# Two layers of two transformer-like blocks on one Trainium2 core: the recurrence's solution eight heads at a time, and the embedding's end in pieces

## The reference, cut to what matters

```python
def step(state, inp):                      # state S[i (value), j (key)], one per head
    r_t, w_t, k_t, v_t, a_t, b_t = inp
    sa = einsum('bhij,bhj->bhi', state, a_t)
    state = state * w_t[:, :, None, :] + sa[..., None] * b_t[:, :, None, :] + v_t[..., None] * k_t[:, :, None, :]
    y_t = einsum('bhij,bhj->bhi', state, r_t)
    return state, y_t
```

```python
gate = sigmoid(rms_norm_2(h, g[6]) @ ple_w_gate[i])
h = h + rms_norm_2(gate * (p[i] @ ple_w_proj[i]), g[7])
```

## Time and profile before

| | us |
|---|---|
| median of three runs | 2233.99 |
| the profiled execution | 2235.59 |
| its span (first to last instruction shown) | 2233.80 |
| TensorE busy | 2150.1 |
| DVE busy | 1525.5 |
| ACT busy | 1151.3 |
| POOL busy | 354.3 |

### The profile page before, as it was taken

The page is one execution under the profiler, slowest core; times in us unless marked ns, Lnnn a source line. Parts: engine busy times, 40 slices in busy tenths (PEclk is TensorE's granted clock), DMA queues, the critical chain, the costliest instruction groups (busy, mean ns, idle before and its releaser), DMA issues.

```text
span 2233.8 us, 40296 instructions
## 1 busy us (share of the span) xinstructions
PE 2150.1 (96%) x14196; PEld 1837.4 (82%) x14196; DVE 1525.5 (68%) x2386; ACT 1151.3 (52%) x1965; POOL 354.3 (16%) x469
## 2 busy tenths in 40 slices
PE   8999899999999899999999999998999899989997
PEld 7888678888888778888887988887888688868886
DVE  6667956667667866666667757667766785767666
ACT  5546645555456555555545454546544543245445
POOL 1111111112111011121110001111111012301111
PEclk9999999999999999999999999999999999999999
DMA  6555426555555345546556446555655340115653
GB/s 246 195 196 178 134 97 204 186 180 188 187 187 187 104 133 191 193 160 198 187 199 230 147 160 202 193 195 195 198 197 186 128 143 13 60 67 188 197 186 111
DMA packets 104115, 375.61 MB, mean 168 GB/s; under 512 B 11696, under 2 KB 12208, under 8 KB 104016
## 3 DMA queue, kind: packets, MB, share of 16 engines
q1 hardware_dynamic: 104016, 374.24, 50.5%
HBM read 373.15 MB, written 1.05 MB: 168 GB/s over the span
## 4 chain that ended last, share of the span: by engine, by line
PE 83%; DVE 9%; ACT 4%; issue 2%; POOL 1%; DMA 1%; SPq 0%; DVEq 0%; ACTq 0%; POOLq 0%
PE bank L846 27%; PE bank L850 14%; PE bank L186 12%; PE bank L187 11%; PE bank L188 11%; DVE w_lo L180 3%; PE bank L1997 2%; DVE work L1361 1%; PE bank L376 1%; ACT w_hi L173 1%; ACT act L435 1%; DMA work<-pt_dram 1%; ACT work L424 0%; DVE act L545 0%; DVE work L575 0%
## 5 line engine op out<-in xcount | busy, mean ns | idle before, releaser
L846 PE MATMUL bank<-act,w_hi 128*128 128x512 f32 x2816 | 709.9, 394 | 2.2 <-ACT w_hi L173 1.1
L846 PEld LDWEIGHTS bank<-act,w_hi 128*128 128x128 f32 x2816 | 520.1, 190 | 106.0 <-DVE act L545 2.6
L760 DVE TENSOR_TENSOR w_lo<-raw,w_hi 128x1024 fp32r<-128x1024 f32 x432 | 503.0, 1220 | 3.4 <-ACT w_hi L751 0.2
L751 ACT ACTIVATE w_hi<-raw 128x1024 fp32r<-128x1024 f32 x432 | 425.0, 1050 | 2.2
L850 PEld LDWEIGHTS bank<-act,w_lo 128*128 128x128 f32 x2816 | 385.3, 191 | 27.9
L850 PE MATMUL bank<-act,w_lo 128*128 128x256 f32 x2816 | 393.5, 283 | 0.0
L180 DVE TENSOR_TENSOR w_lo<-raw,w_hi 128x1024 fp32r<-128x1024 f32 x248 | 295.2, 1221 | 69.3 <-ACT w_hi L173 69.3
L816 DVE TENSOR_TENSOR work<-bank,work 128x256 f32<-128x256 f32 x176 | 74.9, 426 | 387.2 <-ACT work L778 387.2
L793 POOL TENSOR_TENSOR work<-work,rb 128x256 f32<-128x256 f32 x176 | 130.0, 739 | 1047.8 <-DVE work L813 1045.7
L186 PE MATMUL bank<-w_hi,g_hi 128*128 128x512 f32 x704 | 277.3, 394 | 0.9 <-DVE w_lo L180 0.9
L187 PE MATMUL bank<-w_lo,g_hi 128*128 128x512 f32 x704 | 276.0, 392 | 0.0
(11 more groups left out here) (276 smaller groups left out, 2280.9 us busy)
## 6 DMA issues: line engine op xcount, KB each, us to landing
raw<-w_dram SPq DMA_DIRECT2D x680, 512.0 KB, 4.4
work<-rows_dram SPq DMA_DIRECT2D x13, 512.0 KB, 6.4
work<-rrows_dram SPq DMA_DIRECT2D x5, 512.0 KB, 3.3
x<-x_dram SPq DMA_DIRECT2D x2, 512.0 KB, 4.3
out<-x SPq DMA_DIRECT2D x4, 256.0 KB, 2.1
work<-g_dram SPq DMA_DIRECT2D x1, 640.0 KB, 9.6
work<-dist_dram SPq DMA_DIRECT2D x2, 256.0 KB, 5.5
work<-ws_dram SPq DMA_DIRECT2D x1, 512.0 KB, 8.1
```

Of the source, the lines that this page charges most:

```text
L751: nc.scalar.activation(c.w_hi[:, n % RING, :], c.raw[:, n % RING, :], ACT.Copy).then_inc(c.hi_ready, 1)
L760: nc.vector.tensor_tensor(c.w_lo[:, n % RING, :], c.raw[:, n % RING, :], c.w_hi[:, n % RING, :].bitcast(F32), ALU.subtract).then_inc(c.lo_ ...
L846: nc.tensor.matmul(bank[:, :], c.w_hi[:, slot(m), k * P:(k + 1) * P], c.act[:, k, :, :], start=k == 0, stop=False)
```

## The change

In the solution, eight heads (all of one half) are handled together, in two halves instead of four groups. Only M is kept; its transpose is made in each level by four 128x128 transposes per half (`turned`), copied out of PSUM by ACT, and for t = 0 half of it by DVE. The order of the products is over all four quadrants (`quarters`). The grams of b and of k are taken with r and a together, 128 wide. In the embedding, the first token half of the last unit has a mark of its own, and squares, gains and means move into the embedding's stage; `Finish` becomes a kind of `Join`. The first ACT instruction has another function.

```diff
-        nc.scalar.activation(c.small[:, 508:509], c.ident[:, 0:1], ACT.Copy)
+        nc.scalar.activation(c.small[:, 508:509], c.ident[:, 0:1], ACT.Silu)
```

The embedding, and what it calls (in `Join`; `square_y` is the old loop's activation for one quarter):

```diff
+    def mean_y(self, dve, i):
+        t = self.order[i][0]
+        dve.wait_ge(self.s["y_squares"].sem, self.s["y_squares"].at(i + 1))
+        self.sum_parts(self.y_root, self.y_parts, t, EPS / self.by ** 2, self.s["y_mean"])
+    def gain_y(self, dve):
+        i = self.y_gained
+        self.y_gained += 1
+        t, h = self.order[i]
+        if i == 0:
+            dve.wait_ge(self.c.row_in, 16 * self.gain_number)
+        self.quarter_there(dve, i + 1)
+        nc.vector.tensor_tensor(self.gained(t, h), self.sources(t, h), self.gain[...], ALU.mult)
...
                 product_a(c, pe, first + 2 + h * 4 + k, k, 4, [gate(0, h), gate(1, h)], 0,
-                          join.tile_there if h == 0 else None)
+                          join.tile_there if h == 0 else None, s["first"])
...
         for h in range(2):
-            unit_done(c, act, first + 5 + 4 * h)
             for t in range(NT):
+                if t == 0:
+                    act.wait_ge(s["first"].sem, s["first"].at(h + 1))
+                else:
+                    unit_done(c, act, first + 5 + 4 * h)
                 nc.scalar.activation(..., gate(t, h)[:, :], ACT.Sigmoid, scale=...)
+            for t in range(NT):
+                out.square_y(act)
...
                 nc.vector.tensor_tensor(g, g, proj(t, h)[:, :], ALU.mult).then_inc(quad.sem, 1)
+                if h == 1 and t == 1:
+                    out.mean_y(dve, 2)
+                out.gain_y(dve)
+        out.mean_y(dve, 3)
```

The solution, TensorE's queue:

```diff
+    def gram_two(half, bank, left, done):
+        for q, e, ch in quarters(((0, 0), (1, 1), (0, 1), (1, 0))):
+            rows, tok, p = head_rows[e], chunks[ch], 4 * half + q
+            last = nc.tensor.matmul(two_fours(bank[half][e][:, :])[tok, :, q, :], left[rows, p, tok],
+                                    R.raT[rows, :, p, tok], start=True, stop=True)
+    def first_product(half):
+        for q, e, ch in quarters(((0, 0), (1, 1), (1, 0), (0, 1))):
+            last = nc.tensor.matmul(p_bank[half][ch][head_rows[e], ...], X.low_part[tok, cols], X.m[tok, cols], ...)
+    def turned(half):
+        for q in range(4):
+            last = nc.tensor.transpose(m_bank[half][q % 2][:, ...], X.m[:, q * P:(q + 1) * P], c.ident)
+    def second_product(half):
+        for q, e, ch in quarters(((0, 0), (1, 1), (0, 1), (1, 0))):
+            last = nc.tensor.matmul(m_bank[half][e][tok, ...], X.t[rows, ...], X.p1[rows, ...], ...)
+    def p1_and_t(pe, level, half):
+        pe.wait_ge(*at("lows", step + 1))
+        pe.wait_ge(m_made of the level before, or init_made)
+        first_product(half)
+        if not level:
+            pe.wait_ge(*at("kv_made", half + 1))
+        turned(half)
...
+        gram_low(0)
+        gram_two(0, ab_bank, R.bT, "ab_bank")
+        ...                                     # v_out (t = 0) or the last turns (t = 1)
+        gram_low(1)
+        gram_two(0, k_bank, R.kT, "k_bank")
+        pe.wait_ge(*at("low_copied", 2))
+        gram_two(1, ab_bank, R.bT, "ab_bank")
+        pe.wait_ge(*at("init_masked", 1))
+        gram_two(1, k_bank, R.kT, "k_bank")
+        pe.wait_ge(*at("akrk_made", 1))
+        with_values(0)
+        p1_and_t(pe, 0, 0)
+        pe.wait_ge(*at("akrk_made", 2))
+        with_values(1)
+        p1_and_t(pe, 0, 1)
+        for level in range(LEVELS):
+            for half in range(N):
+                pe.wait_ge(p1_made, t_act, and t_dve if t == 0)
+                second_product(half)
+            if level < LEVELS - 1:
+                for half in range(N):
+                    p1_and_t(pe, level + 1, half)
+        # then per half: 16 products with a (four quadrants), 16 of M with the values
```

The other queues of the solution, in their order:

```diff
+    def copy_products(act, level, half):          # ACT
+        act.wait_ge(*at("p1_bank", step + 1))
+        for ch in range(2):                       # two copies, 256 wide
+            last = nc.scalar.activation(X.p1[:, ch * S:(ch + 1) * S], p_bank[half][ch][:, 0:S], ACT.Copy)
+        act.wait_ge(*at("t_bank", step + 1))
+        for i in range(1 + t):                    # one or two copies, 256 wide
+            last = nc.scalar.activation(t_part(half, i), t_in(half, i), ACT.Copy)
+    # ACT: copy_low x2; per half copy_values (two of 512), copy_products(0); then the levels
+    # ACT, t = 1: head.square(act, 0) after copy_products(2, 0)
+    # POOL: per level and half one mask, 512 wide, after the previous level's p1_bank
+    # DVE, per half: two masks of 512, the identity, two masks of 512; then
+        for level in range(LEVELS):
+            if t == 0:
+                for half in range(N):
+                    dve.wait_ge(*at("t_bank", step + 1))
+                    nc.vector.tensor_copy(t_part(half, 1), t_in(half, 1)).then_inc(s["t_dve"].sem, 1)
+            for half in range(N):
+                dve.wait_ge(*at("m_bank", step + 1))
+                for e in range(2):                # two adds, 256 wide
+                    last = nc.vector.tensor_tensor(m, m, fours(m_bank[half][e][:, 0:S]), ALU.add)
+                if t == 1:
+                    head.while_solving(dve, 2 * step)
+                    head.while_solving(dve, 2 * step + 1)
+    # at the end ACT copies two results of 256 per half, DVE one of 512 (R.base, mark "based")
```

More of the change, by code:

```diff
@@ new lines, in eights, with over8, quarters, gram_low @@
+    def eights(u):
+        return u.rearrange("p (h n) -> p h n", n=CHUNK)
+    def over8(mask):
+        return mask.unsqueeze(1).to_broadcast([P, 8, CHUNK])
+    def quarters(order):
+        return [(q, e, ch) for q in range(4) for e, ch in order]
+    def gram_low(half):
+        for q, e, ch in quarters(((0, 0), (1, 1), (0, 1), (1, 0))):
+            rows, tok, p = head_rows[e], chunks[ch], 4 * half + q
+            last = nc.tensor.matmul(low_bank[half][e][tok, q * CHUNK:(q + 1) * CHUNK], R.aT[rows, p, tok],
+                                    R.bT[rows, p, tok], start=True, stop=True)
+        last.then_inc(s["low_bank"].sem, 1)
@@ new lines, in scalar @@
+        for half in range(N):
+            copy_values(act, half)
+            copy_products(act, 0, half)
+        for level in range(1, LEVELS):
+            for half in range(N):
+                copy_products(act, level, half)
+                if t == 1 and level == 2 and half == 0:
+                    head.square(act, 0)
+        for half in range(N):
+            act.wait_ge(*at("final", half + 1))
+            for ch, tok in enumerate(chunks):
+                last = nc.scalar.activation(R.aT[:, 4 * half:4 * half + 4, tok], fours(p_bank[half][ch][:, 0:S]), ACT.Copy)
```

393 lines of the change are left out of this document (180 added, 213 removed).

## The result

The changed kernel takes 2214.37 us, median of 5 runs (2213.09 to 2216.67), beside 2230.57 (2229.67 to 2234.93) for the kernel before on the same chip: ratio 0.9924, interval 0.9909 to 0.9938, so 17 us less (14 to 20). A second set of runs gave 0.9927 (0.9912 to 0.9942). Forecast were 2212, in 2202 to 2226, by a sum of 21.85 us. The time lies in the range. The profiled execution of before lies 5.0 us above this median of before, and the sum came 5 us short, all of it in the two solutions.

A forecast was written before the change was run, and what follows sets the result against it. TensorE, busy 96% of the span, was taken to bound the kernel. Gains 9.5 + 8.2 + 1.75 + 2.25 + 0.15 = 21.85 us off the profiled 2235.59, which stood 1.60 above the median, gave 2212 us, range 2202 to 2226.

The forecast's parts named there:

- Grams and values: Front of each solution, before the levels: level 1 begins at 15.0 us; gain 3.8 us in the first solution.
- Levels: Levels 1 to 4 of the first solution: 4.16 us each, 16.6 instead of 21.0; gain 4.4 us (3.2 to 6.4).
- End: First solution's end, until the state's first product: 4.0 us instead of 5.37; gain 1.3 us.
- Second solution: The recurrence's second solving: 39.4 us instead of 47.56, levels 18.9 as head work delays DVE's adds; gain 8.2 us.
- Embeddings' ends: Last sigmoid to first add of x in both embeddings: 1.75 and 2.25 us less.
- The gain row: Embedding's end: row wanted at about 1536, there by 1538.3, hidden by a margin of 2 us.
- The wait of 0.15: Kernel start: moving the 1.28 us table load to the start removes TensorE's wait behind it, 0.15 us less.
- The clock: Open term: falls to 1.2 GHz after the first solution (up to 3.5 us) and first embedding (3) may stay or go.
- Rival C: Solutions: quadrants don't overlap as in the grams, products stay at 57 ns, only about 4 us gained: 2230; chance 0.07.
- Rival B: Slower: clock at 1.2 GHz through most of both solutions, decisive from 53% of the time, 2253 at all; chance 0.05.
- Rival A: Clock falls inside the solutions part of the time; a quarter of it costs 10 us: 2222; chance 0.20.
- Rival D: More than the sum: neither clock fall comes back and changes of mode cost nothing: 2203; chance 0.08.

The follow-up runs named there:

- two_pads_32: Changed kernel with 32 more products at the first embedding's end and 32 more in the second solution; 2213.33 us, ratio 0.9905 to the kernel before.
- shift128: Changed kernel with 32 more 64x64 products (128 records) where TensorE waits at the first embedding's end; ratio 0.9914 to the kernel before.
- solution_only: Kernel before with only the new solution; embedding's end, last output and first table unchanged; ratio 0.9950 to the kernel before.
- ends_only: Kernel before with only the embedding's end, last output and first table changed, old solution kept; ratio 0.9978 to the kernel before.
- changed_again: The changed kernel itself, unaltered, run again in a later set; 2218.97 us, ratio 0.9927 to the kernel before.
- half_products: Changed kernel with the levels' first and second products over one diagonal pair of quarters only, 8 instead of 16; ratio 0.9889 to the kernel before.
- diagonal_order: Changed kernel with the same products reordered, one diagonal pair of quarters first, then the other; ratio 0.9923 to the kernel before.
- dense_256: Changed kernel with 256 more 64x64 products, no waits among them, at the first embedding's end; 2223.81 us in its one run.
- after: First profiled execution of the changed kernel, unaltered; its solutions took 38.45 and 41.95 us; the kernel's timed ratio to the one before is 0.9924.
- late_head: Changed kernel with the head's DVE operations in the second solution all behind both adds of a level; ratio 0.9913 to the kernel before.

## Why the prediction came out as it did, step by step

- **Grams and values** (15.0): right at 15.01 and 15.27, but with a gap of 0.77 inside the first. Without one it is 14.27 to 14.30 (two_pads_32, shift128), so the layout had 0.7 too much, and that this and the gap cancel is luck. Before, the same stretch held gaps of 2.58 and 0.84. Most of this part's gain of 3.7 is thus a gap that shrank, and not the new order of the work.
- **Levels** (4.16 each): right where no edge falls badly, 4.09 and 3.99 us in the changed kernel and 4.05 to 4.10 in shift128. The change of mode at 0.15 and the product at 30 ns held.
- **End** (4.0): 3.90 in shift128. The 5.38 of the changed kernel hold a gap of 1.26.
- **The step that failed** is the layout of the new queues in order, with prices for products, transposes, copies and handovers: it puts the time that TensorE stands for its instructions at nothing, without a reason, though the kernel before showed such gaps at 1856.02 (2.58 us) and five more places, 7.0 us in all. In the changed kernel they are 3.30 and 1.85 us. The layout without gaps is good to about 1 us for the first solution (34.5 measured, 35.6 forecast); the supply adds 2.1 (solution_only) to 3.9 (the changed kernel). By turning 57 ns products into 30 ns ones the change moved TensorE from about the supply's rate to above it in bursts. Of my 9.5 and 8.2 us for the two solutions 6.7 and 5.6 are in the traces. (My upper bound of 11.9 for the first is 0.4 more than its terms give: 3.8, 6.4 and 1.3.)
- **Second solution**: the levels were forecast at 18.9 and took 21.23; 1.85 of the difference is the gap. TensorE's first wait for DVE was 1.61 in place of 0.75, the next ones 0.5.
- **Embeddings' ends**: 1.95 and 2.36 for 1.75 and 2.25, and 4.9 us (2.5 to 7.1) in the timed runs with the first table. The gain row was waited for until 1536.95, with 5 us to spare to the last sigmoid, so it hid as forecast. The wait of 0.15 is gone.
- **The clock**: "both falls may go or stay". The fall behind the first embedding went from 6.8 us (from 1547.6) to 3.4 (from 1545.9), in the changed kernel as in ends_only. The state steps between the solutions, at a mean clock of 0.77 before and 1.00 after, hold 3.05 us of the profiles' difference:

```profile
1895.60:1910.66 15.06, 15.06 (x288) 14.10 (x289) 7.77 (x12) 2.19 (x4) 0.00 (x0) 0.77 0.12 37
```

```profile
1886.44:1898.45 12.01, 12.01 (x288) 11.24 (x289) 7.77 (x12) 2.19 (x4) 0.00 (x0) 1.00 0.15 46
```

ends_only, with the old solution, crossed the same steps in 12.02 us at 1.00. So the old solution doesn't force this fall, and its 3.05 us can't be credited to the new one. With it the two profiled executions differ by 21.3 us, near my sum, but not for my reasons: the medians differ by 16.2. Two errors, the missing gaps and a profiled execution above the median, offset each other in part, and 2212 stands closer to 2214.37 than the sum deserved.
- **Rival C** (the quadrants don't overlap) is out by the 30 ns. Its price was wrong too: 49 ns, and 2.9 us over both solutions instead of some 17. **Rival B** did not come. **Rival A** came in the second solution of nine of twelve profiled executions; in changed_again it is worth about 2 us, not 10. **Rival D** is out by the 0.14 and 0.16 of a change of mode.

## What to carry over

Where a stretch is made of small products, count instructions as well as nanoseconds: 64 products of 64x64 fill a block, and a block of nothing but such products cost 3.73 us here, though they issue in 1.9. An "issue" gap in the trace of before is a term of the sum, above all when the change makes the instructions around it shorter; number all records ahead of such gaps, semaphore and branch instructions too, and if they share a rest, look to fewer instructions (half_products) or to where the edges fall (shift128's first solution) before a faster order (diagonal_order). A profile tells which part won what; what a change is worth in all comes from the medians, and a part's saving can sit in the clock's luck of one execution.

## Unexpected of the hardware

- TensorE's instruction supply: 256 records every 3.73 us when nothing else holds it up (dense_256), and in the solutions 65 of 65 issue gaps on one rest.
- The gap ahead of record 21273 was 0.72, 0.17, 0.44 and 0.18 us in four executions with the same first solution (after, solution_only, late_head, changed_again): the place is fixed, the length is not.
- TensorE's clock falls at the same place of the same program in one execution and not in another (1.00 and 0.53 from 1932 to 1936, after and changed_again).
- Products over one diagonal took 49 ns each where eight of one diagonal and eight of the other follow each other (diagonal_order), and 61 where eight stand alone (half_products, 0.68 less 0.22 for 16 records); why they differ stays open.
